# A ring of weight chunks in which the rests take the place of the raw chunk, and a slot is reloaded after its use by TensorE

## What is computed

```python
# first block
h = rms_norm(x, norm_mix)
proj = h @ w_in                                # 24 tiles of 128 columns
cat = concat(nsa_mixer, dilated_mixer, stick_breaking_mixer)
x = x + cat @ w_out
h = rms_norm(x, norm_mlp)
x = x + square(relu(h @ w_up)) @ w_down        # 4096 hidden
# second block: layer 0 has the recurrence, layer 1 the convolution
x = x + rwkv7_time_mix(rmsnorm(x))             # r, k, v = three products of mixed inputs
x = x + memory_cross_attention(rmsnorm(x), rmsnorm(mem))   # 256 memory tokens
x = x + conv_ffn(rmsnorm(x))                   # 2 x 2816 hidden
x = x + conformer_conv(rmsnorm(x))
x = x + memory_cross_attention(rmsnorm(x), rmsnorm(mem))
x = x + conv_ffn(rmsnorm(x))
return rmsnorm(x)
```

## Time and profile before

| | us |
|---|---|
| median of 3 runs | 3049.93 |
| lowest, highest | 3048.48, 3050.73 |
| the profiled execution | 3047.94 |
| its span, first to last instruction | 3046.2 |
| TensorE busy | 2677.3 |
| mean granted TensorE clock | 0.91 of full |

### The profile page before, as it was taken

How to read it: one execution, slowest core, us unless ns; L and a number is a source line. 1 busy time by engine, 2 the same in 40 slices (tenths; PEclk the granted TensorE clock), 3 DMA queues, 4 the chain that set the end, 5 groups by cost and what they waited for, 6 DMA issues and landing times. The chain is left out here.

```text
span 3046.2 us, 33071 instructions
## 1 busy us (share of the span) xinstructions
PE 2677.3 (88%) x12202; PEld 2040.8 (67%) x12202; DVE 1157.1 (38%) x2008; ACT 958.7 (31%) x1669; POOL 1060.1 (35%) x626
## 2 busy tenths in 40 slices
PE   5997799999958875899877999999989779999997
PEld 3864457888846524888357778788774577687885
DVE  2011456213032346543231236436377512364261
ACT  3225553212223243122123332322431433322222
POOL 1410236434514101111035244544730353445445
PEclk9986689999979985798779999999999989999998
DMA  3210002323222000000023122332320132223322
GB/s 140 96 64 1 0 1 97 104 90 97 69 76 83 23 16 1 1 1 1 23 97 118 62 69 89 118 97 97 127 95 0 56 110 70 69 83 118 103 97 97
DMA packets 55352, 209.94 MB, mean 69 GB/s; under 512 B 6397, under 2 KB 6525, under 8 KB 54141
## 3 DMA queue, kind: packets, MB, share of 16 engines
q1 hardware_dynamic: 54366, 203.48, 20.2%
q10 hardware_dynamic: 864, 4.85, 0.4%
HBM read 206.20 MB, written 2.10 MB: 68 GB/s over the span
## 5 line engine op out<-in xcount | busy, mean ns | idle before, releaser
L414 POOL TENSOR_TENSOR w_lo<-raw,w_hi 128x1024 fp32r<-128x1024 f32 x362 | 866.3, 2405 | 1247.2 <-ACT w_hi L387 1247.0
L323 PE MATMUL ps<-ahead_hi,w_hi 128*128 128x512 f32 x1216 | 477.0, 392 | 4.6 <-PEq L2859 3.2
L324 PE MATMUL ps<-ahead_lo,w_hi 128*128 128x512 f32 x1216 | 473.8, 390 | 0.0
L325 PE MATMUL ps<-ahead_hi,w_lo 128*128 128x512 f32 x1216 | 473.8, 390 | 0.0
L387 ACT ACTIVATE w_hi<-raw 128x1024 fp32r<-128x1024 f32 x362 | 371.4, 1049 | 228.9 <-PE ps L325 196.2
L323 PEld LDWEIGHTS ps<-ahead_hi,w_hi 128*128 128x128 f32 x1216 | 228.7, 188 | 55.7 <-issue 6.2
L324 PEld LDWEIGHTS ps<-ahead_lo,w_hi 128*128 128x128 f32 x1216 | 228.7, 188 | 48.2 <-issue 1.4
L325 PEld LDWEIGHTS ps<-ahead_hi,w_lo 128*128 128x128 f32 x1216 | 228.7, 188 | 48.1
L523 DVE TENSOR_TENSOR x_stream<-x_stream,ps 128x512 f32<-128x512 f32 x80 | 55.0, 687 | 469.6 <-PE ps L325 469.6
L323 PE MATMUL ps<-ffn_a_hi,w_hi 128*128 128x512 f32 x352 | 142.7, 405 | 10.5 <-POOL w_lo L414 8.0
L324 PE MATMUL ps<-ffn_a_lo,w_hi 128*128 128x512 f32 x352 | 141.3, 401 | 0.0
(11 more groups left out here) (414 smaller groups left out, 4915.6 us busy)
## 6 DMA issues: line engine op xcount, KB each, us to landing
raw<-in_wall SPq DMA_DIRECT2D x368, 512.0 KB, 3.5
x_stream<-in_x SPq DMA_DIRECT2D x1, 2048.0 KB, 9.1
cw<-in_cmp_w SPq DMA_DIRECT2D x1, 2048.0 KB, 7.3
mem<-in_mem ACTq DMA_DIRECT2D x2, 1024.0 KB, 6.6
out_y<-x_stream SPq DMA_DIRECT2D x1, 2048.0 KB, 6.3
dist<-in_consts ACTq DMA_DIRECT2D x1, 1748.5 KB, 6.9
lora_a<-in_lora_a SPq DMA_DIRECT2D x1, 1152.0 KB
gwb<-in_lora_b SPq DMA_DIRECT2D x1, 1024.0 KB
```

The lines of the kernel that those rows point to most:

```text
L323: pe.matmul(out, hi, src.hi[:, t, 0:width], start=first, stop=False)
L324: pe.matmul(out, hi, src.lo[:, t, 0:width], start=False, stop=False)
L325: return pe.matmul(out, lo, src.hi[:, t, 0:width], start=False, stop=last)
L414: e.tensor_tensor(self.w.lo[:, s, :], self.raw[:, s, :], as_float(self.w.hi[:, s, :]), ALU.subtract).then_inc(lo_r.sem, 1)
```

## The change

`raw` and `w.lo` become one ring: `w.lo` is laid over `raw`, so the rests of a chunk are written over its raw weights. The slot is then free only when TensorE has used the chunk. SyncE's load of chunk m therefore waits for `chunk_used` of chunk m-4 in place of `weights_lo` of chunk m-4. When a ring opens, four chunks are loaded instead of six. The rings of the first two openings are placed by hand behind a fence tile, and the third takes 16 KB less of each partition. ScalarE's, GpSimd's and TensorE's instructions stay as they are.

```diff
--- before.py
+++ after.py
@@ -218,20 +218,18 @@
 def open_ring(k, stack, n_chunks, arena=None):
 
     if arena is None:
-        k.raw = stack.enter_context(k.tile("raw", [P, RING, 1024], F32))
-        k.w = Split(stack, k, "w", RING, 1024)
-    else:
-        k.raw, k.w = arena.tile("raw", RING, 1024), arena.split("w", RING, 1024)
+        arena = Arena(k, k.above())
+        stack.enter_context(k.tile("fence", [P, 2 * RING * 1024 + 16], F32))
+    at = arena.at
+    k.raw, k.w = arena.tile("raw", RING, 1024), Halves(arena.tile("w_hi", RING, 1024, dtype=F32R), None)
+    k.w.lo = Arena(k, at).tile("w_lo", RING, 1024, dtype=F32R)
     k.first, k.limit = k.chunk, k.chunk + n_chunks
     hi_r, lo_r = k.sig("weights_hi", "weights_lo")
     slots = k.slots()
     with k.nc.Block() as block:
         @block.sync
         def _(sp):
-            for n in range(RING + AHEAD):
-                if n >= RING:
-
-                    sp.wait_ge(lo_r.sem, lo_r(n - RING + 1))
+            for n in range(RING):
                 sp.dma_start(k.raw[:, n % RING, :], k.wall[k.first + n]).then_inc(slots[n % RING].sem, 16)
 
         @block.scalar
@@ -280,7 +278,7 @@
         self.n_groups, N = m_tiles // 4, m_tiles * self.per
         self.chunk, self.c0 = k.chunk, k.chunk - k.first
         self.n_split = min(N, k.limit - k.chunk - AHEAD)
-        self.n_load = min(N, k.limit - k.chunk - AHEAD - RING)
+        self.n_load = min(N, k.limit - k.chunk - RING)
         self.ending = self.n_split < N
         self.raw, self.w, self.slots = k.raw, k.w, k.slots()
         k.chunk += N
@@ -292,14 +290,13 @@
             k.advance(kt, "fed")
 
     def sync(self, sp):
-        lo_r = self.marks[3]
-        ahead = AHEAD + RING
+        used = self.marks[0]
 
         def load(i, j):
 
-            sp.wait_ge(lo_r.sem, lo_r(i * RING + (j + 1 + AHEAD)))
-            s = (j + self.c0 + ahead) % RING
-            at = self.chunk + j + ahead
+            sp.wait_ge(used.sem, used(i * RING + (j + 1)))
+            s = (j + self.c0) % RING
+            at = self.chunk + j + RING
             source = self.k.wall[at + i * RING] if isinstance(i, int) else \
                 self.k.wall[bass.ds(i * RING + at, 1)].rearrange("o p n -> (o p) n")
             sp.dma_start(self.raw[:, s, :], source).then_inc(self.slots[s].sem, 16)
@@ -2842,14 +2839,14 @@
     zs = Arena(k, low).split("z", KD, T)
     rwkv(k, a, low, zs)
 
-    top = Arena(k, nc.sbuf_usable_end // 64 * 64 - 4 * (3 * RING * 1024 + 2 * KD * T + 4 * T))
+    top = Arena(k, nc.sbuf_usable_end // 64 * 64 - 4 * (2 * RING * 1024 + 2 * KD * T + 4 * T))
     open_ring(k, None, k.n_chunks - k.chunk, top)
     k.ahead = top.split("ahead", KD, T)
     tmp = Scratch(top.tile("sqr", 2, T), top.tile("x_gained", 2, T))
     late = Arena(k, low + 4 * (9 * KD * T // 2 + KD * T // 4 + 128))
     mem = late.tile("mem", KD, MEM)
     ub = Arena(k, late.at - 4 * KD * MEM).tile("ffn_u", 4, T + 2)
-    assert late.at <= top.at - 4 * (3 * RING * 1024 + 2 * KD * T + 4 * T) and low + 4 * (9 * KD * T // 2 + KD * T // 4) > 0
+    assert late.at <= top.at - 4 * (2 * RING * 1024 + 2 * KD * T + 4 * T) and low + 4 * (9 * KD * T // 2 + KD * T // 4) > 0
 
     def load_memory(e):
         e.dma_start(mem[:, :, :], a["mem"]).then_inc(k.sig("memory_loaded").sem, 16)
```

## The result

The changed kernel takes 3077.51 us (median; 3073.32 to 3083.91, 4 runs) against 3050.33 us of the kernel before (4 runs): a ratio of 1.0088, 95% interval 1.0067 to 1.011. It is slower by 27.2 us (0.9%). Its profiled execution took 3077.79 us with a span of 3076.1 us, against 3047.94 and 3046.2 us before: the two traces differ by 29.9 us.

The account below looks back on a forecast made before the run. TensorE, busy 88% of the span, was taken as the bound. First groups 16.0, starts of k and v 5.4, clock 9.8 and openings -1.1 made +30.1 us on the 3049.93 us median: 3080.0 us, range 3075 to 3084.

Parts of the forecast that it names:

- Steady stretches: Chunks behind the first groups: three whole chunks in hand cover load, rounding and rests, so the cost is zero.
- the room: Long 256-column memory stretches: 1.3 us of slack before TensorE needs a chunk, of which the later rounding takes 0.6 us.
- The rival with the short ring: Memory stages: late landings stop TensorE 0.5 us for each of 24 chunks, +12 us, 3092 us; chance 0.12.
- First groups: End of the first group in six fed stages: chunk 4 comes 2.5 us later in four, 3.0 in two; 16.0 us.
- Starts of k and v: Chunk 3's late load delays the operand behind it, so TensorE starts 2.7 us later in each stage; 5.4 us.
- the shift: Start of k and v: chunk 3 lands 1.65 us late with the operand's rounding queued behind it; 1.7 us each.
- the port effect: Start of k and v: VectorE stands still while GpSimd works; without it the sum would be 2.0 us smaller.
- The rival that the late start costs nothing: Start of k and v: TensorE starts later but meets no low clock; 3074.6 us, 5.4 less; chance 0.07.
- Clock: Low clock after six longer first-group stops: 2.3 us each, less 4.0 already lost; 9.8 us, bounds 5.0 to 12.8.
- Openings: Opening of the ring, three times: loads five and six go away, 0.4 us earlier each; -1.1 us.

Follow-up runs that it names:

- the spread kernels: Changed kernel with first-group products reordered so chunk 0 is used earlier, 3038.85 us; the same plus chunk 3 rounded later and tiles placed as before the change, 3030.33 us.
- placement as before: Changed kernel with the fence enlarged so that later tiles lie where they lay in the kernel before: 3078.69 us.
- rests of their own: Changed kernel with late loads and four-load openings kept, but the rests in a separate ring, placed as in the kernel before: 3079.08 us.
- ScalarE's order: Changed kernel, but in stages r, k and v ScalarE rounds chunk 3 after the operand's first two tiles: 3074.64 us.
- GpSimd held back: Changed kernel, but in r, k and v GpSimd starts chunk 3's rests only after VectorE has made the operand's first rest: 3078.69 us.
- The filler: Changed kernel with spare products (20 of 512 columns or 48 of 256) into an unused bank behind each fed stage's first group: 3067.72 us.
- The kernel before with the spread: Kernel before, with each fed stage's first group taking its last four input tiles (six with 256 columns) output tile by output tile: 3025.24 us.

## Why the prediction was right

The forecast was 3080.0 us, the measured median 3077.51; the sum of +30.1 us stands against +29.9 us between the two traces and +27.2 between the medians. The mechanism was right. That the sum lies within 0.2 us of the traces is partly luck: a term that was missed (placement, 3.4 us) stands against one that came out smaller in this trace (the clock, by 2.1 us), and parts that the forecast says nothing of differ by 3 us and more. By its own steps:

- *Steady stretches: nothing.* Right. Behind the first groups the memory stages have no stop in the changed kernel. ScalarE waits 0.3 to 0.5 us there for each load, and the room took it. The rival with the short ring fell. Apart from the second stop of the spread kernels, a late load was seen to cost something there once: 0.4 us in the second layer of the variant with spare products, where the load took 4.7 us to land; two stops of 0.3 us in the last feed-forward layer of two variants have no counterpart in the kernel before.
- *First groups: 16.0 us.* The six stops grew by 2.4, 2.4, 2.5, 2.3, 3.0 and 3.1 us, 15.5 in all. From the first copy, which marks the use, to the rounding of chunk 4 it was 3.6 to 3.7 us, as assumed. The prediction also gave an estimate of 3.2 us for a load, from the Trainium skill ("DMA: Bandwidth & Descriptors", section "Anatomy of one DMA — SWDGE (gpsimd) path"). By its heading that section is on transfers that GpSimd issues, and SyncE issues these: none landed in less than 3.3 us.
- *Starts of k and v: 5.4 us.* 2.6 us each, 5.3 in all. The split was near as well: I had put 1.7 us to the shift and 1.0 us to the port effect, and it was 1.8 and 0.8 us. The rival that the late start costs nothing fell with the two spread kernels: 4.5 us came back when it was taken away.
- *Clock: 9.8 us.* Right in kind, since all six stops are followed by 1.2 GHz. Chunk 4 took 0.8, 1.5, 1.4, 1.4, 2.5 and 0.0 us longer than before, 7.7 us before rounding. The size changes from one execution to the next: in the four other traces with the same six stops the same sum is 10.9 and 10.8 (placement as before, and rests of their own), 9.9 (ScalarE's order) and 7.4 us (GpSimd held back). So 9.8 us was no worse than one execution can tell. The filler, which gives back all of it, the part already lost before included, measured 10 us against 11.7 expected.
- *Openings: -1.1 us.* TensorE's stops there shortened by 0.5, 0.5 and 0.4 us.
- *What was missed: placement.* +3.4 us in the MLP of the trace. I had asked only whether the in-place write costs time, not what moves when a ring shrinks.

These terms make 15.5 + 5.3 + 7.7 - 1.4 + 3.4 = 30.5 us. The rest, -0.6 us, is the sum of larger parts, most of them in stretches whose instructions the change leaves as they were: the mixers took 3.3 us less, the recurrence 3.6 us more (3.2 with the opening behind it), and the queries of the first layer 1.7 us less, since in the kernel before their first 25 products met a low clock (7.6 us against 6.0). The mixers, before and after:

```profile
176.70:460.50 283.80, 229.76 (x1096) 143.91 (x1097) 96.65 (x259) 143.12 (x378) 58.78 (x99) 0.75 0.03 10
```

```profile
179.60:460.10 280.50, 224.39 (x1096) 141.14 (x1097) 96.41 (x259) 142.68 (x378) 58.80 (x99) 0.77 0.03 10
```

The same 1096 products ran at a mean clock of 0.75 and 0.77. The kernel before with the spread, which has the same instructions and placement here as the kernel before, took 278.6 us for the mixers at 0.79, and 523.2 us for the recurrence with its opening, against 519.5. Over all ten traces the mixers took 278.6 to 283.8 us and the recurrence 518.8 to 524.9 us, and neither goes with the load on use or with the placement. So differences of 3 to 5 us in these two stretches come without any change to them. That such parts make the spread of 16 us between executions of the kernel before is an argument from these rows and was not tested. For the recurrence the mean clock is 0.77 in both of the first two traces, and what makes its spread stays open.

## What to carry to other kernels

Sharing a slot's memory between two steps moves the moment when it can be loaded, and the price lies not in the steady loop, with its chunks in reserve, but where several chunks are used up at one moment. Look for those places, lay the latency of load and preparation beside the work that TensorE has left there, and add the low clock that follows a stop of this length. A reordering that spreads the uses over time is worth more than the buffers: it saved 39 us in the changed kernel and 27 us in the one before.

## What the runs showed of the hardware

- Without a single idle moment, 384 products ran 0.9% slower (88.0 against 87.2 us, both at full clock) after tiles allocated behind the rings had been moved by 16 KB less a pad in the on-chip memory, and at the old speed when moved back.
- VectorE and GpSimd with two on-chip inputs each hold one another up for whole instructions, in both directions: 0.69 us became 2.42 or 2.87 for VectorE, and 2.40 became 2.82 for GpSimd.
- Twenty spare products in a stop of 5.3 us kept the next 25 at 2.4 GHz: 5.7 us, not 7.1.
- Loads of 512 KB issued some 0.7 us apart landed later one after another: in the changed kernel's r, four of them took 3.4, 4.3, 5.6 and 6.1 us from issue, where 3.5 is the median.
